# Attention rounds: where the transposes of the two softmax tiles stand among the gate products

## What is computed

```python
for gi, (window, dilation) in enumerate(((128, 1), (512, 4), (2048, 16))):      # 4 heads each
    logits = jnp.where(valid, q @ k.T * E ** -0.5 - slopes * distance, -jnp.inf)
    lse = logsumexp(logits); o = exp(logits - lse) @ v
wts = softmax(lses over the 3 groups); y_b = sum(wts * outs)
gate_a, gate_b = split(sigmoid(h @ w_gate + b_gate))
merged = gate_a * (y_a @ w_branch_a) + gate_b * (y_b @ w_branch_b)
```

## Time and profile before

| | us |
|---|---|
| median of 3 runs | 921.97 (921.3 to 922.11) |
| the profiled execution | 922.39 |
| its span in the profile | 920.6 |
| PE busy | 906.5 |
| DVE busy | 547.0 |
| ACT busy | 450.0 |
| POOL busy | 435.2 |

### The profile page before, as it was taken

The page is one execution under the profiler, slowest core; times in us unless marked ns, Lnnn a source line. Parts: engine busy times, 40 slices in busy tenths (PEclk is TensorE's granted clock), DMA queues, the critical chain, the costliest instruction groups (busy, mean ns, idle before and its releaser), DMA issues.

```text
span 920.6 us, 16015 instructions
## 1 busy us (share of the span) xinstructions
PE 906.5 (98%) x6621; PEld 747.6 (81%) x6621; DVE 547.0 (59%) x834; ACT 450.0 (49%) x729; POOL 435.2 (47%) x198
## 2 busy tenths in 40 slices
PE   8999999999999999999999999999999999999996
PEld 6887888897777788888888888888888888888886
DVE  4223799215455448879445666676676657669535
ACT  6355453255454644634444544444443444346747
POOL 3453444443233526346523566566555555649540
PEclk9999999999999999999999999999999999999998
DMA  7442333332221100226425324242233252320222
GB/s 229 135 112 66 94 89 92 92 92 76 63 61 35 28 26 25 71 83 213 139 80 146 96 71 158 69 135 80 83 115 91 72 157 70 117 89 23 94 91 92
DMA packets 115166, 86.34 MB, mean 94 GB/s; under 512 B 2852, under 2 KB 100022, under 8 KB 115094
## 3 DMA queue, kind: packets, MB, share of 16 engines
q1 hardware_dynamic: 114904, 85.24, 31.1%
q10 hardware_dynamic: 190, 0.08, 0.0%
HBM read 83.21 MB, written 2.10 MB: 93 GB/s over the span
## 4 chain that ended last, share of the span: by engine, by line
PE 95%; DVE 2%; ACT 1%; DMA 1%; issue 1%; POOL 0%; SPq 0%; DVEq 0%; ACTq 0%
PE bank L654 20%; PE bank L655 19%; PE bank L656 19%; PE bank L719 4%; PE bank L721 4%; PE bank L720 4%; PE bank L1263 4%; PE bank L1261 4%; PE bank L1264 4%; PE bank L1006 2%; PE bank L859 1%; PE bank L962 1%; PE bank L1003 1%; DMA xs<-in_x_dram 1%; PE bank L886 1%; PE bank L973 1%
## 5 line engine op out<-in xcount | busy, mean ns | idle before, releaser
L634 POOL TENSOR_TENSOR w_lo<-raw,w_hi 128x1024 fp32r<-128x1024 f32 x114 | 277.8, 2437 | 395.5 <-ACT w_hi L1324 383.8
L654 PE MATMUL bank<-hT_hi,w_hi 128*128 128x512 f32 (+1 forms) x720 | 282.0, 392 | 0.1
L656 PE MATMUL bank<-hT_hi,w_lo 128*128 128x512 f32 (+1 forms) x720 | 277.0, 385 | 0.0
L655 PE MATMUL bank<-hT_lo,w_hi 128*128 128x512 f32 (+1 forms) x720 | 276.9, 385 | 0.0
L1324 ACT ACTIVATE w_hi<-raw 128x1024 fp32r<-128x1024 f32 x113 | 119.9, 1061 | 252.4 <-issue 139.9
L654 PEld LDWEIGHTS bank<-hT_hi,w_hi 128*128 128x128 f32 x720 | 135.2, 188 | 28.2 <-DVE hT_lo L2242 0.4
L656 PEld LDWEIGHTS bank<-hT_hi,w_lo 128*128 128x128 f32 x720 | 135.2, 188 | 27.2
L655 PEld LDWEIGHTS bank<-hT_lo,w_hi 128*128 128x128 f32 x720 | 135.3, 188 | 25.0
L2349 DVE SCALAR_TENSOR_TENSOR cbuf<-bank,params,cbuf 128x511 f32<-128x511 f32 x48 | 36.0, 750 | 102.9 <-ACT cbuf L1750 102.7
L1261 PE MATMUL bank<-up_w_hi,mixed_hi 128*128 128x512 f32 x144 | 56.1, 390 | 0.0
L1263 PE MATMUL bank<-up_w_lo,mixed_hi 128*128 128x512 f32 x144 | 56.0, 389 | 0.0
(11 more groups left out here) (340 smaller groups left out, 1586.0 us busy)
## 6 DMA issues: line engine op xcount, KB each, us to landing
raw<-in_w_up_dram SPq DMA_DIRECT2D x48, 512.0 KB, 3.8
raw<-in_w_in_dram SPq DMA_DIRECT2D x33, 512.0 KB, 4.0
quads<-in_w_down_dram SPq DMA_DIRECT2D x24, 512.0 KB, 4.4
raw<-in_w_gate_dram SPq DMA_DIRECT2D x16, 512.0 KB, 4.0
raw<-in_w_out_dram SPq DMA_DIRECT2D x8, 512.0 KB, 4.5
raw<-in_w_ple_gate_dram SPq DMA_DIRECT2D x8, 512.0 KB, 3.8
xs<-in_x_dram SPq DMA_DIRECT2D x4, 512.0 KB, 5.6
raw<-in_w_branch_a_dram SPq DMA_DIRECT2D x4, 512.0 KB, 3.4
```

The source lines that it names most:

```text
L634: nc.gpsimd.tensor_tensor(low(n)[:, :], source(n), high(n)[:, :].bitcast(F32), ALU.subtract).then_inc(*step("pool", ("lo", n)))
L654: nc.tensor.matmul(o, wh, ah, start=first, stop=False)
L655: nc.tensor.matmul(o, wh, al, start=False, stop=False)
L656: return nc.tensor.matmul(o, wl, ah, start=False, stop=last)
```

## The change

In rounds 1 to 6 the PE's list had T(2n), six eighths, T(2n + 1), two eighths. It now has four eighths, T(2n), T(2n + 1), four eighths. In round 7 it had the same order as the others, and now has T(14), T(15), eight eighths. The lists of all other engines stay as they are, and so do all waits, banks and buffers.

```diff
             for n in range(1, 8):
                 if n + 1 < 8:
                     scores(n + 1)
+                if n < 7:
+                    gate_parts(4)
                 transposed_p(2 * n)
-                gate_parts(6)
                 transposed_p(2 * n + 1)
-                gate_parts(2)
+                gate_parts(4 if n < 7 else 8)
                 weighted_values(n)
```

## The result

| | us |
|---|---|
| before, median of 7 runs | 921.49 (920.95 to 922.11) |
| changed, median of 7 runs | 924.34 (922.9 to 925.4) |
| changed to before | 1.0028, 95% interval 1.0018 to 1.0037 |
| the changed kernel's profiled execution | 923.95, span 922.2 |

The change makes the kernel 0.28% slower. Forecast were slower and 924.1 us, with a range from 922.9 to 926.0; the range held. The changed kernel's times are also spread wider, over 2.5 us in place of 1.2.

What follows compares the result with a forecast made beforehand. The PE, busy 98% of the span, was taken to bound the kernel. Round 7's wait of +2.3 us and seam of -0.2, rounds 1 to 6 nothing, gave +2.1 us: 924.1 us against a 921.97 median, range 922.9 to 926.0.

Steps and rivals of the forecast that it cites:

- What bounds the kernel: Whole kernel: PE busy 98% of the span; its attention stage has no wait to remove.
- The wait of T(15): Round 7: T(15), right behind T(14), waits for P(15) from ACT and DVE; PE idle 2.3 us.
- Rounds 1 to 6 at zero: Rounds 1 to 6: no waits, seams unchanged, cost 0; ends -0.25 and +1.5 us.
- a sign that it was wrong: Rounds 1 to 6 becoming shorter would mean that two T together cost less than counted.
- The seam of round 7: Round 7: one passage from eighths to transposes and back is gone, -0.2 us.
- the feared waits: Rival: rounds 1 to 6 wait too, for the gate's bank or P(2n + 1); up to 1.5 us, 925.6; chance 0.10.
- The clock: Rival, round 7: clock falls in the wait, three eighths at half pace, 2.1 us more, 926.2; chance 0.10.
- The argument against it: Against a clock fall in round 7: full clock through a 0.7 us wait, and 2.3 us is barely as long.
- the idleness at the kernel's end: Behind the kernel's last product: the granted clock fell to the lower level in less than 2.5 us.
- The sign that the prediction gave: Attention stage, round 7: granted clock stays at 1.00 from 270 to 285 us.
- Is it given back?: Line 1003, behind the stage: idle 0.69 us could absorb delay; taken as nothing. Rival with larger seam gain: 923.4, chance 0.10.
- The sum: Whole kernel: -0.2 seam, +2.3 wait, rounds 1 to 6 nothing: +2.1 us, 924.1 us, 0.23% slower.

Runs made afterwards that it cites:

- e5: Changed kernel with ACT's exponential of tile 15 ahead of moving gate 6 and DVE's scaling of tile 15 ahead of `yb_rest`; 920.84 us, 0.9988 of before.
- e2: Kernel before with only round 7 changed (T(14), T(15), eight eighths), rounds 1 to 6 in the old order; 924.81 us, 1.0034 of before.
- e1: Changed kernel with round 7 back in the old order (T(14), six eighths, T(15), two eighths); 920.83 us, 0.9992 of before.
- e7: Changed kernel with all seven rounds as four eighths, T(2n), two eighths, T(2n + 1), two eighths; 923.81 us, 1.0023 of before.
- e3: Changed kernel with round 7 also as four eighths, both T, four eighths, like the other rounds; 921.53 us, 0.9996 of before.
- e6: Changed kernel with round 7 as two eighths, T(14), T(15), six eighths; 921.87 us, 1.0 of before.
- e8: The changed kernel run again unaltered, for more executions with their mean clock; 924.73 us, 1.003 of before.
- e4: Changed kernel with nine extra 512-column products, into a bank nobody reads, between T(14) and T(15); 924.05 us, 1.0027 of before.
- e9: The edits of e5 and e4 together on the changed kernel: tile 15 served early, plus the nine extra products; 923.96 us, 1.0024 of before.

## Why the prediction was right, and where its sizes were off

**What bounds the kernel.** Right. The PE had no wait in the stage, and what the rounds lost came out at the end almost in full.

**The wait of T(15).** Right in place, chain and size: 2.24 us, forecast 2.3; T(15) starts 4.11 us behind `weighted_values(6)`, forecast 4.17. The link that counts is in the lists of ACT and DVE, shown by e5: with the same PE list and tile 15 served first, the wait is gone. e2 shows that rounds 1 to 6 have no part in it.

**Rounds 1 to 6 at zero.** Wrong in size. They gained 0.61 us together, more than the -0.25 us that was given as the end. The prediction had named this as a sign that it was wrong: two T together cost less than it counted. The step took it that the number of passages is all that a seam costs. But T behind T saves more than T behind scores: 20 transposes together take 0.78 us, before 0.46 + 0.45. e1 shows the gain and e7 its reverse. The seam of round 7 was counted too small by the same step: without a wait the round is 0.41 us shorter than before (7.85 us in e5 against 8.26), not 0.2. None of the feared waits (P(2n + 1), the copies, the gate's bank) came in these rounds; the bank did make a wait in round 7 of e3 and e6, where no scores stand ahead. The prediction checked it only for the rounds that have them.

**The clock.** The mechanism was named and priced at 2.1 us, with a chance of 0.10, and the sum had nothing for it. This was the larger mistake. It came in the profiled executions of the changed kernel, e2 and e8, and by time and mean clock in 10 of 13 executions of the changed kernel. Its price is 1.6 us (7.79 against 6.19 us in e4). The argument against it, that the clock had stayed up through 0.7 us, and that 2.3 us is barely as long as the idleness at the kernel's end, weighed too much. The sign that the prediction gave, a granted clock of 1.00 from 270 to 285 us, reads 0.89. The idleness at the kernel's end was one reading, 2.35 us; the eleven profiles have 2.0 to 5.2 us there, so one execution doesn't give a length below which a wait is safe. After 2.24 us of idleness and another 0.5 to 1.2 us of work, the PE was granted 1.2 GHz in place of 2.4 for eight products or so, and 2.4 again after that. The Trainium skill, "TensorE: Matmul & The Clock Gate", section "Part 1: The HAM clock gate", says that idleness brings the clock to half. The trace agrees: the granted clock was 0.50 behind the wait.

**Is it given back?** Right: the idle 0.69 us at line 1003 is 0.70 us now.

**The sum.** Forecast +2.1: a wait with its seam at +2.1, the rest nothing. Measured in the rounds +3.03: the wait with its seam +2.04, the clock +1.60, rounds 1 to 6 -0.61. (The profiled spans differ by 1.6 us only: in the changed kernel's execution the rounds began 0.55 us earlier, and the part behind them was 0.88 us shorter, with none of the long intervals of e9's section.) The measured difference of the medians, +2.85, is 0.75 us over the forecast +2.1. That 924.1 lies only 0.24 us under the measured 924.34 is in part luck, twice: the two errors are of opposite sign, and the median of the kernel before, 921.97 in three runs, was 921.49 in seven. The executions whose clock stayed up are 1.4 to 1.7 us over before. That is under the 1.8 us which the prediction took for the least that can be told, but the intervals here are only some 0.9 us to either side.

## What to carry to other kernels

When filler is moved on a full engine, look up for each item behind it when its data is ready, counted from the last event that starts the producer's chain; the last round, which has lost one of its members, needs a count of its own. A wait of the matrix engine of some 2 us can cost more than its length: here the half clock behind it added 1.6 us in most executions. And if an item comes early, first see whether the producers' lists can serve it earlier: one item moved up on ACT and one on DVE turned 0.3% slower into 0.1% faster.

## What was not expected of the hardware

- Transposes of 64 x 64 behind others of their kind save 0.12 to 0.15 us a pair of tiles against one behind scores and one among 512-column products; an extra passage costs 0.35 us (e1, e7). With transposes of 128 x 128 the pair saves nothing (round 4: +0.06 us).
- 2.24 us of idleness were enough for the lower clock in all three profiled executions that had them, and, going by time and mean clock, in most of the others but not in all; 0.7 us and 0.5 us were not in any profiled execution. At the kernel's start, 1.8 us were enough in one (e8), and 1.5 us at the same place were not in the profile of the kernel before.
- The clock fell after the wait, not in it: 1.2, 0.7 and 0.5 us behind the start of T(15) (changed, e2, e8). Behind the kernel's last product it fell after 2.0 to 5.2 us.
- The stage of short matmuls behind has intervals that are up to 0.9 us over the usual for nothing that the profile names; their places and sizes differ from profile to profile, and with them go totals that are up to 1 us over what the rounds explain (e4, e9).
